# RMS norms read from PSUM, their roots taken straight from the sums' bank, and layer parameters turned in another stage

## The reference, cut to what matters

```
for i in range(2):
    f = swiglu_ffn(rmsnorm(x, ffn1_norm_pre[i]), ffn1_w_in[i], ffn1_w_out[i])
    x = x + 0.5 * rmsnorm(f, ffn1_norm_post[i])
    h = rmsnorm(x, mix_norm_pre[i])
    ...                                     # the mixer: convolutions, gated delta rule, gates
    x = x + rmsnorm(y, mix_norm_post[i])
    f = swiglu_ffn(rmsnorm(x, ffn2_norm_pre[i]), ffn2_w_in[i], ffn2_w_out[i])
    x = x + 0.5 * rmsnorm(f, ffn2_norm_post[i])
rmsnorm(x, w) = x * rsqrt(mean(x * x) + 1e-6) * w
```

## Time and profile before

| what | us |
|---|---|
| median of three runs | 3099.71 |
| the profiled execution | 3098.85 |
| its span, first to last instruction | 3097.2 |
| busy: TensorE matmuls | 2691.1 |
| busy: VectorE | 1643.6 |
| busy: ScalarE | 810.7 |
| busy: GpSimd | 560.0 |

### The profile page before, as it was taken

How to read it: one execution, slowest core, us unless ns; L and a number is a source line. 1 busy time by engine, 2 the same in 40 slices (tenths; PEclk the granted TensorE clock), 3 DMA queues, 4 the chain that set the end, 5 groups by cost and what they waited for, 6 DMA issues and landing times.

```text
span 3097.2 us, 34544 instructions
## 1 busy us (share of the span) xinstructions
PE 2691.1 (87%) x14238; PEld 2184.6 (71%) x14238; DVE 1643.6 (53%) x3236; ACT 810.7 (26%) x1334; POOL 560.0 (18%) x539
## 2 busy tenths in 40 slices
PE   7998999887996997999887997999897777777776
PEld 7996887876996996888786997788686323333232
DVE  5443963634445444575543554424522777777874
ACT  4431113222433431103221342143202121112211
POOL 0000000000000000000000000000002777777775
PEclk8999998898998998999798998999898888888888
DMA  5575983002553555995003453543143999999997
GB/s 194 180 167 92 149 148 109 1 28 95 183 182 102 182 177 96 149 145 151 14 1 109 141 186 98 163 129 130 41 136 116 395 374 394 389 386 382 392 389 301
DMA packets 324717, 557.14 MB, mean 180 GB/s; under 512 B 16200, under 2 KB 245586, under 8 KB 324562
## 3 DMA queue, kind: packets, MB, share of 16 engines
q1 hardware_dynamic: 250834, 286.48, 34.8%
q0 software_dynamic: 73728, 268.47, 22.4%
HBM read 553.85 MB, written 1.05 MB: 179 GB/s over the span
## 4 chain that ended last, share of the span: by engine, by line
PE 73%; POOL 10%; DVE 7%; issue 4%; DMA 3%; ACT 2%; SPq 0%; DVEq 0%; ACTq 0%
PE bank L320 30%; PE bank L346 8%; PE bank L347 8%; PE bank L348 8%; PE bank L966 6%; PE bank L1988 5%; POOL proj L1932 5%; POOL expert_u_rows L1928 5%; DMA expert_u_rows<-in_peer_u,gdn_conv 3%; PE bank L776 2%; PE bank L547 2%; DVE branch L565 1%; ACT residual L1973 1%; PE bank L763 1%; DVE stat L560 1%
## 5 line engine op out<-in xcount | busy, mean ns | idle before, releaser
L320 PE MATMUL bank<-operand,weights 128*128 128x256 f32 x3456 | 753.5, 380 | 3.8 <-DVE operand L565 3.8
L320 PEld LDWEIGHTS bank<-operand,weights 128*128 128x128 f32 x3456 | 658.2, 191 | 95.9 <-issue 5.4
L1988 PE MATMUL bank<-proj,residual 128*128 128x512 f32 x1024 | 519.8, 672 | 190.1 <-ACT residual L1973 190.1
L1988 PEld LDWEIGHTS bank<-proj,residual 128*128 128x128 f32 x1024 | 218.9, 217 | 490.4 <-issue 297.3
L346 PE MATMUL bank<-operand_hi,weights_high 128*128 128x256 f32 x1408 | 403.5, 287 | 20.6 <-DVE operand_lo L596 20.6
L347 PE MATMUL bank<-operand_lo,weights_high 128*128 128x256 f32 x1408 | 402.1, 286 | 0.0
L348 PE MATMUL bank<-operand_hi,weights_low 128*128 128x256 f32 x1408 | 402.0, 285 | 0.0
L1941 DVE CUSTOM_DVE_ANT_0 expert_u_rows<-expert_u_rows,branch 128x1024 f32<-128x1024 f32 x256 | 306.2, 1224 | 164.9 <-DMA expert_u_rows<-in_peer_u,gdn_conv 159.6
L340 DVE TENSOR_TENSOR weights_low<-weights,weights_high 128x1024 fp32r<-128x1024 f32 x264 | 308.1, 1221 | 130.9 <-ACT weights_high L332 130.9
L628 POOL TENSOR_TENSOR residual<-residual,branch 128x512 f32<-128x512 f32 x12 | 17.2, 1437 | 1900.4 <-DVE branch L565 1900.4
L1932 POOL DMA_INDIRECT proj<-in_peer_v,gdn_conv x256 | 290.4, 1134 | 78.0 <-issue 68.6
(11 more groups left out here) (356 smaller groups left out, 3016.5 us busy)
## 6 DMA issues: line engine op xcount, KB each, us to landing
weights<-in_ffn_w_in SPq DMA_DIRECT2D x88, 1024.0 KB, 5.0
weights<-in_mix_w_in SPq DMA_DIRECT2D x64, 1024.0 KB, 11.8
weights<-in_ffn_w_out SPq DMA_DIRECT2D x44, 1024.0 KB, 5.0
weights<-in_w_in SPq DMA_DIRECT2D x24, 1024.0 KB, 5.3
weights<-in_cnv_w_o SPq DMA_DIRECT2D x8, 1024.0 KB, 5.1
weights<-in_gdn_w_o SPq DMA_DIRECT2D x8, 1024.0 KB, 5.2
weights<-in_mix_w_out SPq DMA_DIRECT2D x8, 1024.0 KB, 5.1
weights<-in_peer_w_q SPq DMA_DIRECT2D x8, 1024.0 KB, 5.2
```

The source lines that it names most:

```text
L320: ins = t.matmul(out, raw[:, k, q * P:(q + 1) * P], x[:, k, :], start=(k == 0), stop=(k == KT - 1))
L1988: ins = t.matmul(m.bank[2 * p + half][:, :], K.diag[p][:, s, :], K.v[p][:, s, half * 512:half * 512 + 512], start=(s == 0), stop=(s == GRO ...
```

## The change

Post norms square the branch straight from banks 4 to 7, pair by pair, as each bank is complete; for that the last `out` block of an FFN works through its outputs column by column, and the mixer's last four blocks write banks 4 to 7. The copies to `branch` are gone. VectorE gathers the squares of the four pairs into one pair, and TensorE sums that pair in two matmuls. The scaling too reads the banks. Pre norms leave the adding of tile pairs out: TensorE sums all eight squared tiles. The root is taken by ScalarE from bank 3 with scale and epsilon inside the instruction, and VectorE takes the reciprocal of the root behind it. A small square root on one column is put earlier in ScalarE's program. The parameters of layer l+1 (or of the block) are loaded, turned and copied out around the second FFN of layer l. The core of the diff:

```
+def scalar_squares(X, m, S, n, src, tmp, ready):
+    for i in range(4):
+        X.act.wait_ge(*ready[i])
+        S.squared.by(X.scalar.square(tmp[:, pairs_of(i), :], src(i)), n, i)
+
+def tensor_sums(X, m, S, n, tmp):
     X.bank_free(3)
-    for i in range(4):
-        X.pe.wait_ge(*S.halved.at(n, i))
-        ins = X.tensor.matmul(m.bank[3][:, 0:NT], m.ones[:, :], tmp[:, 2 * i, :], start=(i == 0), stop=(i == 3))
+    for k in range(KT):
+        X.pe.wait_ge(*S.squared.at(n, k // 2))
+        ins = X.tensor.matmul(m.bank[3][:, 0:NT], m.ones[:, :], tmp[:, k, :], start=(k == 0), stop=(k == KT - 1))
     S.summed.by(ins, n)
-    X.free[3] = [S.inverse.at(n, "mean")]
+    X.free[3] = [S.std.at(n)]
...
+def scalar_root(X, m, S, n):
+    X.act.wait_ge(*S.summed.at(n))
+    S.std.by(X.scalar.activation(m.stat, m.bank[3][:, 0:NT], ACT.Sqrt, bias=m.eps[:, 0:1], scale=1.0 / (KT * P)), n)
+
+def scalar_sqrt_table(X, m, n):
+    X.scalar.activation(m.eps[:, n + 1:n + 2], m.eps[:, 0:1], ACT.Sqrt)
+
+def vector_root(X, m, S, n):
+    X.dve.wait_ge(*S.std.at(n))
+    S.inverse.by(X.vector.reciprocal(m.stat, m.stat), n)
+    X.dve.wait_ge(*S.inverse.at(n))
...
+def y_tiles(m):
+    return lambda i: m.two(4 + i)
...
+def tensor_post_norm(X, m, S, n):
+    X.bank_free(3)
+    X.pe.wait_ge(*S.gathered.at(n, 3))
+    for q in range(2):
+        ins = X.tensor.matmul(m.bank[3][:, 0:NT], m.ones[:, :], m.spare[:, q, :], start=(q == 0), stop=(q == 1))
+    S.summed.by(ins, n)
+    X.free[3] = [S.std.at(n)]
+    for b in range(4):
+        X.free[4 + b] = [S.scaled.at(n, b)]
+
+def vector_post_norm(X, m, S, n, gain):
+    X.dve.wait_ge(*S.squared.at(n, 0))
+    for i in range(1, 4):
+        X.dve.wait_ge(*S.squared.at(n, i))
+        if i > 1:
+            X.dve.wait_ge(*S.gathered.at(n, i - 1))
+        S.gathered.by(X.vector.tensor_tensor(m.spare[:, 0:2, :], m.spare[:, 0:2, :], m.spare[:, pairs_of(i), :], ALU.add), n, i)
+    vector_root(X, m, S, n)
     for i in range(4):
-        vector_scale_two(X, m, S, n, i, m.x, gain, m.operand)
+        vector_scale_two(X, m, S, n, i, y_tiles(m), gain, m.y)
+        if i % 2:
+            X.dve.wait_ge(*S.scaled.at(n, i))
+            S.added_dve.by(X.vector.tensor_tensor(m.x[:, pairs_of(i), :], m.x[:, pairs_of(i), :], m.y[:, pairs_of(i), :], ALU.add), n, i)
...
     # tensor_ffn: the last out block
+        last = j == FF - 1
+        for c, k in [(c, k) for c in range(KT) for k in range(2)] if last else [(c, k) for k in range(2) for c in range(KT)]:
...
+            if last and k == 1 and c in (1, 3, 5):
+                S.y_bank.by(ins, stage, c // 2)
...
     # vector_ffn: the copies behind an FFN
-    for b in range(4):
-        S.y_out.by(v.tensor_copy(m.y[:, pairs_of(b), :], m.two(4 + b)), stage, b)
...
     # the programs of the engines
 def tensor_program(X, m, S, K):
     tensor_input(X, m, S)
+    tensor_params(X, m, S, 0)
     for l in range(LAYERS):
-        tensor_params(X, m, S, l)
...
         tensor_mixer(X, m, S, l)
-        tensor_root(X, m, S, ("post", l), m.operand)
-        tensor_root(X, m, S, ("pre2", l), m.y)
+        tensor_post_norm(X, m, S, ("post", l))
+        tensor_params(X, m, S, l + 1)
+        tensor_pre_norm(X, m, S, ("pre2", l))
         tensor_ffn(X, m, S, ("ffn2", l), split_at(S, ("pre2", l)))
...
 def vector_program(X, m, S, K):
...
         vector_split_norm(X, m, S, ("pre2", l), g(4))
+        vector_params(X, m, S, l + 1)
         vector_ffn(X, m, S, ("ffn2", l))
...
 def sync_program(X, m, S, K, io):
...
         sync_mixer(X, m, S, io, l)
+        if l + 1 < LAYERS:
+            sync_layer_params(X, m, S, io, l + 1)
+        else:
+            sync_block_params(X, m, S, io)
         sync_ffn(X, m, S, ("ffn2", l), l, io["ffn2_w_in"], io["ffn2_w_out"])
```

More of the change, by code:

```diff
@@ L370, in tensor_blocks @@
     for b in range(first, first + n):
-        tensor_block(X, m, S, b, x, ready if b == first else ())
+        tensor_block(X, m, S, b, x, ready if b == first else (), b % BANKS)
         X.free[b % BANKS] = [out.at(b)]
@@ new lines, in pool_post_norm, with added_at, scalar_pre_norm, tensor_pre_norm @@
+def pool_post_norm(X, m, S, n):
+    for i in (0, 2):
+        X.pool.wait_ge(*S.scaled.at(n, i))
+        S.added_pool.by(X.gpsimd.tensor_tensor(m.x[:, pairs_of(i), :], m.x[:, pairs_of(i), :], m.y[:, pairs_of(i), :], ALU.add), n, i)
+def added_at(S, n):
+    return [S.added_dve.at(n, i) if i % 2 else S.added_pool.at(n, i) for i in range(4)]
+def scalar_pre_norm(X, m, S, n, ready):
+    scalar_squares(X, m, S, n, x_tiles(m), m.operand, ready)
+    scalar_root(X, m, S, n)
+def tensor_pre_norm(X, m, S, n):
+    tensor_sums(X, m, S, n, m.operand)
@@ L611, in split_at @@
     return [S.x_low.at(n, i) for i in range(4)]
[L614 to L632, removed]
 def sync_ffn(X, m, S, stage, l, w_in, w_out):
@@ L660, in tensor_ffn @@
         hi, lo, x = wide(m.high[i % HIGHS]), wide(m.low[s]), m.split_gated
[L661 to L665, removed]
+        last = j == FF - 1
+        for c, k in [(c, k) for c in range(KT) for k in range(2)] if last else [(c, k) for k in range(2) for c in range(KT)]:
+            at = slice(c * P, (c + 1) * P)
+            ins = tensor_three(X, m.bank[4 + c // 2][:, c % 2 * NT:(c % 2 + 1) * NT], hi[:, k, at], lo[:, k, at], x.hi[:, k, :],
+                               x.lo[:, k, :], j == 0 and k == 0 and c % 2 == 0, last and k == 1, skip=True)
+            if last and k == 1 and c in (1, 3, 5):
+                S.y_bank.by(ins, stage, c // 2)
         S.used.by(ins, b)
-    for b in range(4):
-        X.free[4 + b] = [S.y_out.at(stage, b)]
 def scalar_ffn(X, m, S, stage):
@@ L697, in vector_ffn, with ffn_y_at @@
                                              ALU.subtract), stage, j)
-    w.wait_ge(*S.used.at(first + len(FFN_ORDER) - 1))
-    for b in range(4):
-        S.y_out.by(v.tensor_copy(m.y[:, pairs_of(b), :], m.two(4 + b)), stage, b)
-def y_at(S, stage):
-    return [S.y_out.at(stage, b) for b in range(4)]
+def ffn_y_at(S, stage):
+    return [S.y_bank.at(stage, b) for b in range(3)] + [S.used.at(RING.first[stage] + len(FFN_ORDER) - 1)]
 def vector_softplus(X, step, exp, n, x, out, a, b):
@@ L1259, in tensor_mixer @@
     finish(tensor_blocks(X, m, S, ("gdn_o", l), 4, m.conv, S.out_dve, [S.delta_dve.at(l, "o", i) for i in range(4)]))
-    finish(tensor_blocks(X, m, S, ("mix_o", l), 4, x, S.out_act, [S.branch.at(l, i) for i in range(4)]))
+    for i in range(4):
+        tensor_block(X, m, S, RING.first["mix_o", l] + i, x, [S.branch.at(l, k) for k in range(4)] if i == 0 else (), 4 + i)
 def scalar_mixer(X, m, S, l):
@@ L1314, in mix_out_at @@
 def mix_out_at(S, l):
-    return [S.out_act.at(RING.first["mix_o", l] + b) for b in range(4)]
+    return [S.used.at(RING.first["mix_o", l] + b) for b in range(4)]
 def rev(a, d):
@@ L2102, in scalar_program @@
         scalar_ffn(X, m, S, ("ffn1", l))
-        scalar_root(X, m, S, ("post1", l), m.y, m.operand, y_at(S, ("ffn1", l)))
-        scalar_norm(X, m, S, ("mix", l), added_at(S, ("post1", l)))
+        scalar_sqrt_table(X, m, 1 + 3 * l)
+        scalar_post_norm(X, m, S, ("post1", l), ffn_y_at(S, ("ffn1", l)))
+        scalar_pre_norm(X, m, S, ("mix", l), added_at(S, ("post1", l)))
         scalar_mixer(X, m, S, l)
-        scalar_root(X, m, S, ("post", l), m.y, m.operand, mix_out_at(S, l))
+        scalar_sqrt_table(X, m, 3 + 3 * l)
+        scalar_post_norm(X, m, S, ("post", l), mix_out_at(S, l))
         for i in range(AHEAD):
@@ L2110, in scalar_program @@
         scalar_ffn(X, m, S, ("ffn2", l))
-        scalar_root(X, m, S, ("post2", l), m.y, m.operand, y_at(S, ("ffn2", l)))
-    scalar_norm(X, m, S, "norm1", added_at(S, ("post2", LAYERS - 1)))
+        scalar_sqrt_table(X, m, 2 + 3 * l)
+        scalar_post_norm(X, m, S, ("post2", l), ffn_y_at(S, ("ffn2", l)))
+    scalar_pre_norm(X, m, S, "norm1", added_at(S, ("post2", LAYERS - 1)))
     scalar_block_two(X, m, S)
-    scalar_norm(X, m, S, "norm2", block_added_at(S))
+    scalar_sqrt_table(X, m, 7)
+    scalar_pre_norm(X, m, S, "norm2", block_added_at(S))
     scalar_scores(X, m, S, K)
@@ L2137, in vector_program @@
         vector_split_norm(X, m, S, ("pre2", l), g(4))
+        vector_params(X, m, S, l + 1)
         vector_ffn(X, m, S, ("ffn2", l))
[L2139 to L2142, removed]
+        X.dve.wait_ge(*columns_at(S, l + 1))
+        vector_post_norm(X, m, S, ("post2", l), g(5))
+    vector_pre_norm(X, m, S, "norm1", m.block_w[:, 0:8])
     vector_block_two(X, m, S)
-    vector_norm(X, m, S, "norm2", m.block_w[:, 96:104])
+    vector_pre_norm(X, m, S, "norm2", m.block_w[:, 96:104])
     vector_counting(X, m, S, K)
```

90 lines of the change are left out of this document (38 added, 52 removed).

## The result

The changed kernel takes 3052.16 us, the median of four runs (3049.98 to 3054.78), beside 3101.55 us for the kernel before (3097.43 to 3105.29): a ratio of 0.9841, 95% interval 0.9824 to 0.9858, or 49.4 us less. The forecast was 3065.6 in a range of 3053 to 3079: the way was right, the size was not, and the time lies 0.8 us under the range.

The account below looks back on a forecast made before the run. TensorE was taken as the bound (73% of the span), with only its gaps between stages movable. Terms 17.6 + 3.7 + 6.3 + 7.1 + 0.0 - 0.6 = 34.1 us gave 3064.8 profiled, 3065.6 as median; range 3053 to 3079.

Parts of the forecast that it names:

- Where its matmuls run back to back the change touches nothing: Stretches of back-to-back TensorE matmuls, such as inside the FFNs: 0 gained; only gaps between stages can move.
- The norms' part: Gaps around all norms together: 17.6 + 3.7 + 6.3 + 7.1 + 0.0 - 0.6 = 34.1 us gained.
- Post norms: Six, last matmul to scaling: 4.8 us each; 17.6 us gained behind four FFNs, 3.7 behind two mixers.
- The port: Forecast: GpSimd's 1.0 us hold moves from scaling to residual add. Rival (0.11): scaling stays held, 4 us lost, 3069.6.
- Pre norms' sums: TensorE's sixteen records take 6.2 us, clock rising on the way; mixers' norms and norm1 gain 6.3 us together.
- T: Start of a post norm's scaling, from which the following times are counted in us.
- Between the layers: One pre norm: scaling at T+12.3 against 19.37 before, VectorE's weight cutting ending later than the sums; 7.1 us gained.
- Ahead of the second FFN: Two pre norms: scaling 4.1 us earlier each, but first matmuls wait for VectorE's copies, 8.2 lost in all; sum 0.0.
- the wait ahead: Before the second FFN's pre norm sums: parameter turning waits for all four scaled pairs, T+4.6; sums start at T+5.6.
- First norm, norm2: Kernel start: scaling at 27.4 against 26.71, -0.6 us (between +1 and -2); norm2: 0, within 1.5 either way.
- the rivals: Low clock (0.16, 3078), port held (0.11, 3069.6), banks signalled late (0.04, 3073), parameters late (0.04, 3139), better than forecast (0.05, 3057).
- the parameters were not late: Rival (0.04): next parameters not landed when TensorE reaches their turning, all sums queued behind; 74 us lost, 3139.

## Why the prediction was wrong

The step that failed stands in the part on what bounds the kernel: "Where its matmuls run back to back the change touches nothing". It does, by where the tiles lie: the FFNs' steps went from 17.28 to 16.96 us, 13.8 us off the FFNs' spans and so over a quarter of the 49.4. This is shown by the two kernels that carry the shift alone and the change without it. Without the shift the change takes 3068.1 us, 2.5 from the forecast of 3065.6; beside the kernel before on its chip that is 35.1 us less, where 34.1 were forecast. The norms' part was thus nearly right as a sum, with one term off by 3.5 us, as told below. Nothing in the trace of before could have given its price, but the diff shows a tile allocated ahead of all operands, and I read that line as memory and not as a change to the hottest matmuls.

The steps on the norms, one by one:

- **Post norms.** Forecast 4.8 us, measured 4.87 to 4.94, at the high clock level as argued from the 1.66 us gap (here 1.50 and 1.41). Right.
- **The port.** The hold moved from the scaling to the residual add, as weighed; none of the 48 scalings from banks is held. The Trainium skill's rule ("SBUF — State Buffer", "SBUF: two separate sides") stands: with one input in a bank the operation passes GpSimd, and the add with both inputs in SBUF waits for it. The trace agrees: no such scaling over 484 ns, and the adds 1073 to 1089 ns in place of 690.
- **Pre norms' sums.** Sixteen records forecast at 6.2 us with a rise on the way: 5.1 to 6.6 measured, depending on when the clock rises. Scaling at T+11.6: 11.5, 11.8 and 12.0. Right.
- **Between the layers.** 7.1 forecast, 7.7 measured. The cutting is the last wait, as forecast: the root is there at T+8.6, and the reciprocal starts at T+9.9, when the cutting ends. But the cutting began at T+5.4 and not T+5.7, and behind it come only reciprocal and scaling: scaling at T+11.7, not 12.3.
- **Ahead of the second FFN.** 0.0 forecast, 3.5 gained. The mechanism and its price were right (6.61 and 6.18 us from scaling to first matmul, 6.7 and 6.3 forecast, released by the copies). Mis-sized was the wait ahead: I had the turning wait for all four pairs in both layers. It waits bank by bank, so that in layer 1, with two tiles, it is done before the first square and the sums start at T+3.0, and scaling at T+11.7 in place of 14.1. There the sums are no longer the last wait: the root is there at T+9.1 and the reciprocal waits for VectorE's cutting until T+9.9. In layer 0 the sums start at T+4.7 in place of 5.6, and scaling at T+13.3.
- **First norm, norm2.** -0.6 and 0 forecast, -0.7 and 0.1 measured.

Of the rivals none came true; the parameters were not late either: the last of their loads was issued at 688.6, and their turning, which began at 728.1, waited for the scaling alone. The range left out the case in which stretches that the change doesn't name get faster; 3053 was its end, and 3052.2 the time.

## What to carry to other kernels

A new tile in the middle of an allocation is an edit to every operand behind it: compare the pitch of the hottest instruction before and after, and test the shift by itself before crediting the idea. Move a step into a place where both of its engines wait, and see what is queued behind its last wait: the same copies cost 4.2 us (layer 0) and 3.5 us (layer 1) behind the operand's cutting, and nothing ahead of the post norm's root. And what an addition on a shared engine costs is set by what stands in front of it, not by its length.

## What the runs showed of the hardware

The rate of the FFNs' fp32r matmuls (128x128 weights, 256 columns) depends on where weights and operands lie against one another in SBUF. A matmul comes every 120.0 ns where all start at the same remainder by 128 bytes (both remainders that were tried, 0 and 64), and every 118.1, 117.8, 116.3 and again 118.1 ns in the four layouts where some are off by 64 or 32. In the last of these, with 32 bytes, the fourth FFN is an exception: 122.4 ns, unexplained. Over this kernel's 6336 such matmuls the best layout seen is worth 23 us.

The step is steadier than its parts. In the changed kernel, over some 300 matmuls of each kind, the one with high operand and high weights comes 117.2 ns behind the one ahead of it, low operand and high weights 118.9, high operand and low weights 117.3 in the first FFN; in the third FFN these are 113.3, 119.2 and 120.8, and in both the three sum to the same 353 ns. In the kernel before all three take 120.0. So these pitches don't tell which reads meet.
